# The inverse inside the recurrence, computed on 32-row diagonal blocks instead of whole 128-row matrices

## The chip, the core and the metric

One core of one Trainium2 chip. The metric is the device time of one execution in microseconds (us); three executions of the kernel before are shown. The engines are PE (TensorE), DVE (VectorE), ACT (ScalarE), POOL (GpSimd) and SP (which issues the weight loads).

## The reference, cut to what matters

The program is a two-layer model on 256 tokens of width 1024. The change touches only the first mixer, a recurrence with 8 heads of width 64:

```python
def step(S, inp):
    r_t, k_t, v_t, w_t, kk_t, a_t = inp
    sa = jnp.einsum('bhvk,bhk->bhv', S, -kk_t)
    S = (S * w_t[:, :, None, :]
         + sa[..., None] * (kk_t * a_t)[:, :, None, :]
         + v_t[..., None] * k_t[:, :, None, :])
    y = jnp.einsum('bhvk,bhk->bhv', S, r_t)
    return S, y
```

`sa` of a token depends on the `sa` of all tokens before it. Over a chunk of 128 tokens this is a linear system with a strictly triangular 128x128 matrix L for each head: sa = (I - L)^-1 rhs. The kernel computes that inverse and then works by matrix products. All else (projections, retention, gates, feed-forward, the second layer) is untouched.

## The kernel before

The 256 tokens are two chunks, n = 0 and n = 1. For each chunk, `mats` holds four masked 128x128 products of each of the 8 heads: PE makes them in two matmuls of 256 columns a head (L659, L660) into banks 0 to 3 in turn, and DVE masks each bank into `mats` (L2189). L itself in the other orientation comes from four matmuls for each half of the heads into banks 4 and 5 (L666); DVE masks them (L2197).

The inverse grows by doubling: level 0 is written down directly (DVE L2197 to L2203), and level k joins neighbouring blocks of 2^k rows to blocks of 2^(k+1). Levels 1 to 4 (`WHOLE` is 5) work on whole matrices:

- POOL masks `mats` to what level k needs, `lk` (L1253), in two halves of four heads.
- PE multiplies `lk` by `inv` into banks 4 and 5 (L678, 8 matmuls), ACT copies the result to `t1` (the helper `copy`, L1432).
- PE multiplies `invT` by `t1`, and `t1` by `invT` (L688, 16 matmuls, banks 0 to 3); DVE adds the four banks to `inv` and `invT` (L2213), 512 columns each.

Half q = 0 of the heads fills its banks before half q = 1 starts, so ACT and DVE begin on the first half while PE is at the second. Levels 5 and 6 work on blocks of 32 and 64 rows: matmuls of 32x32 and 64x64 (L700, L711, L718), copies by ACT L1534, adds by DVE L2222 and L2225.

Between the steps PE runs other work: `dense(place)` issues `quarters` of the retention projections, and a quarter is six matmuls of 128x128x512 (L443 to L445). The table `QUARTERS` gives one quarter behind each `t` step and one behind each `x` step, and five behind the start. DVE and ACT have a `dense(place)` too: ACT copies results out (L1432) and makes the rounded upper part of a weight unit (L1333), DVE the remainder (L1903), once every four quarters. In the second chunk DVE also runs a piece of the rotary embedding in each level (L2144 to L2162), in the first the angles (L2039 to L2061).

Waits on PSUM go by bank: `take` makes PE wait until the bank's last content was read, `full` makes a reader wait for PE, `emptied` waits for a reader. Each engine works through its own list in the order of the code.

## Time and profile before

| | us |
|---|---|
| median of three executions | 935.45 |
| lowest, highest | 935.07, 939.02 |
| the profiled execution | 936.12 |
| span of the profiled execution, first to last instruction | 934.3 |
| PE busy | 899.6 (96% of the span) |
| DVE busy | 678.2 (73%) |
| ACT busy | 510.9 (55%) |
| POOL busy | 81.4 (9%) |
| mean granted TensorE clock, as a share of full speed | 0.993 |

The span leaves out what lies ahead of the first and behind the last instruction (1.8 us here). A matmul of fp32 operands shows as two MATMUL rows and two LDWEIGHTS rows in the trace. "Idle before" is what the engine waited, and behind the arrow stands whose work ended that wait.

### The profile page before, as it was taken

What the parts mean: (1) busy time and instruction counts of PE and PEld (TensorE: products, weight loads), DVE (VectorE), ACT (ScalarE), POOL (GpSimd) and SP (SyncE); (2) the same over time, 40 slices, a digit from 0 to 9 for tenths busy, and PEclk for the clock granted to TensorE, in tenths of its full rate; (3) what the DMA queues carried; (4) which work ended last, traced back from release to release, by engine and by line L of the source; (5) the groups of instructions that cost most, each with busy time, mean ns of one, the idle gap of its engine ahead of it and who ended that gap; (6) DMA issues with size and microseconds to landing.
All of it is one profiled execution on the core that took longest, in us unless ns stands there. A gap on an engine that the chain in (4) does not pass through costs nothing.

```text
span 934.3 us, 14617 instructions
## 1 busy us (share of the span) xinstructions
PE 899.6 (96%) x5801; PEld 786.6 (84%) x5801; DVE 678.2 (73%) x968; ACT 510.9 (55%) x732; POOL 81.4 (9%) x83
## 2 busy tenths in 40 slices
PE   6999999999999989999999899999999998999998
PEld 5998988988888769999988699988888786878777
DVE  6688737856868678898854668787686777776665
ACT  7863332243535376665643565765565666577553
POOL 6002402300000000000000000007320000000000
PEclk9999999999999989999999999999999999999999
DMA  9543222122555455565555454552323544532231
GB/s 310 171 149 105 92 91 90 47 92 90 195 188 179 149 168 181 189 208 189 183 190 197 153 172 147 185 180 90 112 82 123 176 151 153 204 105 91 91 116 64
DMA packets 80979, 136.63 MB, mean 146 GB/s; under 512 B 3957, under 2 KB 46545, under 8 KB 80912
## 3 DMA queue, kind: packets, MB, share of 16 engines
q1 hardware_dynamic: 78800, 131.17, 42.1%
q0 software_dynamic: 2112, 4.53, 1.6%
q8 instruction: 46, 0.75, 0.3%
q14 instruction: 21, 0.17, 0.1%
HBM read 134.64 MB, written 1.05 MB: 145 GB/s over the span
## 4 chain that ended last, share of the span: by engine, by line
PE 63%; DVE 6%; ACT 6%; issue 3%; DMA 1%; DVEq 0%; ACTq 0%
PE bank L443 18%; PE bank L445 17%; PE bank L444 17%; PE bank L432 3%; DVE lower L1903 2%; ACT upper L1333 2%; PE bank L1112 1%; PE bank L917 1%; PE bank L925 1%; PE bank L1096 1%; DVE arena L2456 1%; ACT arena L1819 1%; DMA loaded<-in_ffn_w_up 1%; DMA loaded<-in_ple_gate_w 1%; ACT arena L1432 1%
## 5 line engine op out<-in xcount | busy, mean ns | idle before, releaser
L1903 DVE TENSOR_TENSOR lower<-loaded,upper 128x2048 fp32r<-128x2048 f32 x122 | 278.6, 2287 | 123.8 <-ACT upper L1333 121.7
L1333 ACT ACTIVATE upper<-loaded 128x2048 fp32r<-128x2048 f32 x122 | 231.9, 1903 | 115.3 <-PE bank L445 99.0
L443 PE MATMUL bank<-xT_upper,upper 128*128 128x256 f32 (+1 forms) x664 | 186.5, 281 | 2.7 <-DVE lower L1895 1.6
L444 PE MATMUL bank<-xT_lower,upper 128*128 128x256 f32 (+1 forms) x664 | 185.0, 279 | 0.0
L445 PE MATMUL bank<-xT_upper,lower 128*128 128x256 f32 (+1 forms) x664 | 184.9, 278 | 0.0
L443 PE MATMUL bank<-upper,xT_upper 128*128 128x512 f32 (+1 forms) x360 | 146.7, 407 | 4.6 <-DVE lower L1903 3.4
L445 PE MATMUL bank<-upper,xT_lower 128*128 128x512 f32 (+1 forms) x360 | 139.9, 389 | 0.0
L444 PE MATMUL bank<-lower,xT_upper 128*128 128x512 f32 (+1 forms) x360 | 139.3, 387 | 0.0
L443 PEld LDWEIGHTS bank<-xT_upper,upper 128*128 128x128 f32 (+1 forms) x664 | 125.1, 188 | 4.1 <-DVE lower L1895 1.8
L444 PEld LDWEIGHTS bank<-xT_lower,upper 128*128 128x128 f32 (+1 forms) x664 | 125.3, 189 | 0.2
L445 PEld LDWEIGHTS bank<-xT_upper,lower 128*128 128x128 f32 (+1 forms) x664 | 125.2, 189 | 0.1
L443 PE MATMUL bank<-upper,split_arena 128*128 128x512 f32 x296 | 120.8, 408 | 2.9 <-DVE split_arena L1968 2.1
L444 PE MATMUL bank<-lower,split_arena 128*128 128x512 f32 x296 | 117.5, 397 | 0.0
L445 PE MATMUL bank<-upper,split_arena 128*128 128x512 f32 x296 | 117.5, 397 | 0.0
L1432 ACT ACTIVATE arena<-bank 128x512 f32<-128x512 f32 (+1 forms) x83 | 46.8, 587 | 94.9 <-PE bank L678 33.2
L443 PEld LDWEIGHTS bank<-upper,xT_upper 128*128 128x128 f32 x360 | 68.1, 189 | 19.8 <-DVE lower L1903 4.5
L445 PEld LDWEIGHTS bank<-upper,xT_lower 128*128 128x128 f32 x360 | 67.7, 188 | 14.9
L444 PEld LDWEIGHTS bank<-lower,xT_upper 128*128 128x128 f32 x360 | 68.0, 189 | 12.2 <-issue 0.5
L443 PEld LDWEIGHTS bank<-upper,split_arena 128*128 128x128 f32 x296 | 56.0, 189 | 17.5 <-DVE lower L1903 2.1
L445 PEld LDWEIGHTS bank<-upper,split_arena 128*128 128x128 f32 x296 | 55.9, 189 | 13.7
L444 PEld LDWEIGHTS bank<-lower,split_arena 128*128 128x128 f32 x296 | 56.0, 189 | 12.5 <-issue 0.5
L432 PE MATMUL bank<-consts,arena 128*128 128x128 f32 (+2 forms) x333 | 49.4, 288 | 15.3 <-DMA arena<-in_norm_mix_pre 4.9
(349 smaller groups left out, 1167.9 us busy)
## 6 DMA issues: line engine op xcount, KB each, us to landing
loaded<-in_w_in SPq DMA_DIRECT2D x26, 1024.0 KB, 5.1
loaded<-in_ffn_w_up SPq DMA_DIRECT2D x22, 1024.0 KB, 5.1
loaded<-in_ssm_in_w SPq DMA_DIRECT2D x20, 1024.0 KB, 5.2
loaded<-in_ffn_w_down SPq DMA_DIRECT2D x11, 1024.0 KB, 4.9
loaded<-in_ssm_out_w SPq DMA_DIRECT2D x8, 1024.0 KB, 4.9
loaded<-in_ple_gate_w SPq DMA_DIRECT2D x8, 1024.0 KB, 5.0
loaded<-in_attn_in_w SPq DMA_DIRECT2D x8, 1024.0 KB, 5.2
loaded<-in_w_branch_ret SPq DMA_DIRECT2D x4, 1024.0 KB, 4.9
```

What stands on the lines that cost most here:

```text
L432: last = pe.transpose(ps[0:n, j * P:j * P + m], a, ident[0:m, 0:m])
L443: mm(out, a[0], b[0], start=start, stop=False)
L444: mm(out, a[0], b[1], start=False, stop=False)
L445: return mm(out, a[1], b[0], start=False, stop=stop)
L917: last = mm(ps[:, P * e:P * e + P], later[:, z % 2, e, :], const("incl"), start=True, stop=True)
L925: last = mm(ps[:, 64 * e:64 * e + 64], wT[:, n, e, :], xd[:, n, 64 * hd:64 * hd + 64], start=True, stop=True)
L1096: last = mm(ps[:, w * e:w * e + w], aqT[r, u, nh * gh * n + e, P * n:P * n + P], akT[r, u, 0:w], start=False, stop=(e == nh - 1))
L1112: last = mm(ps[:, 65 * e:65 * e + 65], aeT[:, z % 2, P * (kt_ * e + s):P * (kt_ * e + s) + P], vv[:, s, 2 * u + o, :], start=(s == 0), sto ...
L1333: A(part(upper, PARTS, n), part(loaded, LOADS, n), ACT.Copy).then_inc(uppers, 1)
L1432: empty(A(dst, ps[0:part_, 0:w], func), key)
L1819: ins = A(asb[:, z % 2, w * e:w * e + w], ps[:, w * e:w * e + w], ACT.Exp, bias=mx[:, z % 2, e:e + 1], scale=rs8[:, n, hd + e:hd + e + 1])
L1903: TT(part(lower, LOADS, n), part(loaded, LOADS, n), part(upper, PARTS, n).bitcast(F32), sub) \
```

## The change

The inverse of each diagonal block of 32 rows needs nothing outside that block. Levels 1 to 4 are now computed on these four blocks alone. `blocks` holds, for each head and packed in 32 columns each, the scratch product `bt1`, the block of L `bdiag`, and the two orientations of the inverse `binv` and `binvT`. Block b lies on partitions 32b to 32b+31 and has a PSUM bank of its own, b.

- PE: L and its transpose on the diagonal blocks come from 64 matmuls with 32 columns and 64 rows of contraction (banks 4 and 5), and they now stand ahead of the matmuls of `mats`. A level is 32 matmuls of 32x32 and then 64 of 32x32, going round the four blocks; each of the four banks is filled by its last matmul.
- DVE: two copies, two masked writes and one add of `unit` make level 0, ahead of the eight `mats` banks. A level's four adds are on 32 partitions and 512 columns each. Level 4 writes into the full-size `inv` and `invT` (`inverses`), which POOL has zeroed; levels 5 and 6 copy where they added.
- ACT: four copies of 32 partitions x 256 columns a level instead of two of 128 x 512.
- POOL: one memset of `inverses`, then the four masks of a chunk in one go, 128 x 256 each, as soon as the two copies of DVE are done.

The core of the diff:

```diff
+                ps = [take(pe, ("L", n, o), 4 + o) for o in range(2)]
+                for p in range(4):
+                    for v in range(2):
+                        for b in ROWS:
+                            for o in range(2):
+                                r = slice(64 * o, 64 * o + 64)
+                                a, x = zr[r, p, n, b], bt[r, p, n, b]
+                                last = mm(ps[o][b, 64 * p + 32 * v:64 * p + 32 * v + 32], x if v else a, a if v else x,
+                                          start=True, stop=True)
...
                 for k in range(1, WHOLE):
-                    for q in range(2):
-                        pe.wait_ge(sem("lk_ready"), 2 * (WHOLE - 1) * n + 2 * (k - 1) + q + 1)
...
-                        for e in range(4):
-                            last = mm(ps[:, P * e:P * e + P], lk[:, 4 * q + e, :], inv[:, 4 * q + e, :],
+                    pe.wait_ge(sem("lk_ready"), (WHOLE - 1) * n + k)
+                    ps = [take(pe, ("t1", n, k, b), b) for b in range(4)]
+                    for hd in range(8):
+                        for b, r in enumerate(ROWS):
+                            last = mm(ps[b][r, 32 * hd:32 * hd + 32], lk[r, k - 1, hd, :], binv[r, hd, :],
                                       start=True, stop=True)
-                        fill(last, ("t1", n, k, q))
+                            if hd == 7:
+                                fill(last, ("t1", n, k, b))
                     dense(("t", n, k))
...
+                    ps = [take(pe, ("x", n, k, b), b) for b in range(4)]
+                    for hd in range(8):
+                        for v, (a, x) in enumerate(((binvT, bt1), (bt1, binvT))):
+                            for b, r in enumerate(ROWS):
+                                c = 64 * hd + 32 * v
+                                last = mm(ps[b][r, c:c + 32], a[r, hd, :], x[r, hd, :], start=True, stop=True)
+                                if hd == 7 and v:
+                                    fill(last, ("x", n, k, b))
                     dense(("x", n, k))
...
                 for k in range(1, LEVELS):
                     if k < WHOLE:
-                        for q in range(2):
-                            copy(t1[:, 4 * q:4 * q + 4, :], ("t1", n, k, q))
+                        for b, r in enumerate(ROWS):
+                            ps = full(act, ("t1", n, k, b))
+                            empty(A(bt1[r, :, :], ps[r, 0:256].rearrange("p (a b) -> p a b", a=8), ACT.Copy), ("t1", n, k, b))
...
+                    if k < WHOLE - 1:
+                        for b, r in enumerate(ROWS):
+                            ps = full(ve, ("x", n, k, b))[r, :].rearrange("p (a v c) -> p a v c", a=8, v=2)
+                            empty(TT(blocks[r, :, 2:4, :], ps, blocks[r, :, 2:4, :], add), ("x", n, k, b))
+                        emptied(ve, *[("x", n, k, b) for b in range(4)])
...
+                pool.wait_ge(sem("diag_blocks"), 2 * n + 2)
                 for k in range(1, WHOLE):
...
+                    pool.tensor_tensor(lk[:, k - 1, :, :], bdiag, const(f"off{k}").unsqueeze(1).broadcast_to([P, 8, 32]),
+                                       ALU.mult).then_inc(sem("lk_ready"), 1)
```

PE's list at one level of the inverse, before (a row's count is in matmuls of the program):

```order
L678 MATMUL bank<-arena 128x128 x8
L443 MATMUL bank<-upper,xT_upper 128x512
L444 MATMUL bank<-lower,xT_upper 128x512
L445 MATMUL bank<-upper,xT_lower 128x512
L443 MATMUL bank<-upper,xT_upper 128x512
L444 MATMUL bank<-lower,xT_upper 128x512
L445 MATMUL bank<-upper,xT_lower 128x512
L688 MATMUL bank<-arena 128x128 x16
```

and now:

```order
L687 MATMUL bank<-arena 32x32 x32
L450 MATMUL bank<-upper,xT_upper 128x512
L451 MATMUL bank<-lower,xT_upper 128x512
L452 MATMUL bank<-upper,xT_lower 128x512
L450 MATMUL bank<-upper,xT_upper 128x512
L451 MATMUL bank<-lower,xT_upper 128x512
L452 MATMUL bank<-upper,xT_lower 128x512
L697 MATMUL bank<-arena 32x32 x64
```

The quarter of retention work between the two steps stays; the steps have four times as many, smaller matmuls.

DVE's list at the start of the first chunk, before:

```order
L1903 TENSOR_TENSOR lower<-loaded,upper 128x2048
L2189 TENSOR_TENSOR arena<-bank,consts 128x512 x8
L2197 TENSOR_TENSOR arena<-bank,consts 128x4x128 x2
L2198 TENSOR_TENSOR arena<-arena,consts 128x1024
L2201 TENSOR_TENSOR arena<-arena,consts 128x1024
L2203 TENSOR_TENSOR arena<-arena,consts 128x1024
L1903 TENSOR_TENSOR lower<-loaded,upper 128x2048
L2213 TENSOR_TENSOR arena<-arena,bank 128x512 x4
```

and now:

```order
L1914 TENSOR_TENSOR lower<-loaded,upper 128x2048
L2203 COPY arena<-bank 128x4x32
L2204 TENSOR_TENSOR arena<-bank,consts 128x4x64
L2203 COPY arena<-bank 128x4x32
L2204 TENSOR_TENSOR arena<-bank,consts 128x4x64
L2207 TENSOR_TENSOR arena<-arena,consts 128x8x64
L2213 TENSOR_TENSOR arena<-bank,consts 128x512 x8
L1914 TENSOR_TENSOR lower<-loaded,upper 128x2048
L2222 TENSOR_TENSOR arena<-bank,arena 32x8x64 x4
```

Level 0 moved from behind the eight `mats` banks to ahead of them, and shrank; the adds of a level keep their number and their 512 columns.

## Rows read from the trace of the kernel before

**Rows 1.** The page, its first line.
```profile
span 934.3 us, 14617 instructions
```

**Rows 2.** Timeline of PE (start, length, line, form, count); both chunks.
```profile
86.61 2.05 PE L678 MATMUL bank<-arena 128*128 128x128 f32 x16 [0.15 <-DVE arena L2203]
...
88.41 0.48 PE L443 MATMUL bank<-upper,xT_upper 128*128 128x512 f32 x1
...
89.89 3.73 PE L688 MATMUL bank<-arena 128*128 128x128 f32 x32
...
93.38 0.48 PE L443 MATMUL bank<-upper,xT_upper 128*128 128x512 f32 x1
...
119.90 0.69 PE L700 MATMUL bank<-arena 32*32 32x32 f32 x32 [0.49 <-DVE arena L2213]
...
159.28 2.05 PE L678 MATMUL bank<-arena 128*128 128x128 f32 x16 [0.15 <-DVE arena L2203]
...
192.53 0.69 PE L700 MATMUL bank<-arena 32*32 32x32 f32 x32 [0.46 <-DVE arena L2213]
```

**Rows 3.** Timeline of PE, levels 5 and 6 of the second chunk.
```profile
194.74 0.60 PE L711 MATMUL bank<-arena 32*32 32x32 f32 x26
195.16 0.22 PE L718 MATMUL bank<-arena 32*32 32x32 f32 x2
...
195.25 0.60 PE L718 MATMUL bank<-arena 32*32 32x32 f32 x27
195.78 0.50 PE L443 MATMUL bank<-upper,xT_upper 128*128 128x512 f32 x1
...
197.91 1.11 PE L700 MATMUL bank<-arena 64*64 64x64 f32 x16 [0.49 <-DVE arena L2225]
```

**Rows 4.** Timeline of PE, start of the second chunk.
```profile
150.14 0.72 PE L666 MATMUL bank<-arena 64*128 64x128 f32 x5
150.59 0.48 PE L659 MATMUL bank<-arena 64*128 64x256 f32 x1
150.69 0.38 PE L666 MATMUL bank<-arena 64*128 64x128 f32 x2
```

**Rows 5.** Timeline of ACT, level 5 of the second chunk.
```profile
193.23 0.78 ACT L1534 ACTIVATE arena<-bank 32x256 f32<-32x256 f32 x2 [4.96 <-PE bank L700]
```

**Rows 6.** Timeline of DVE, levels 5 and 6 of the second chunk.
```profile
196.77 0.43 DVE L2222 TENSOR_TENSOR arena<-bank,arena 32x256 f32<-32x256 f32 x1
197.23 0.42 DVE L2225 TENSOR_TENSOR arena<-bank,arena 32x256 f32<-32x256 f32 x1
...
201.81 0.68 DVE L2225 TENSOR_TENSOR arena<-bank,arena 64x512 f32<-64x512 f32 x1 [0.25 <-PE bank L718]
```

**Rows 7.** Timelines of PE and DVE, start of the first chunk.
```profile
72.78 0.71 PE L659 MATMUL bank<-arena 64*128 64x256 f32 x4
...
79.30 0.50 PE L443 MATMUL bank<-upper,xT_upper 128*128 128x512 f32 x1
...
75.15 3.67 DVE L2189 TENSOR_TENSOR arena<-bank,consts 128x512 f32<-128x512 f32 x6
```

**Rows 8.** Timelines of POOL and DVE, start of the first chunk.
```profile
80.63 3.58 POOL L1253 TENSOR_TENSOR arena<-arena,consts 128x512 f32<-128x512 f32 x2 [65.25 <-DVEq L2193]
...
83.18 2.11 DVE L2201 TENSOR_TENSOR arena<-arena,consts 128x1024 f32<-128x1024 f32 x1
85.32 1.23 DVE L2203 TENSOR_TENSOR arena<-arena,consts 128x1024 f32<-128x1024 f32 x1
```

**Rows 9.** Timeline of DVE, levels 3 and 4 of the second chunk.
```profile
184.13 0.69 DVE L2148 TENSOR_TENSOR arena<-lora 128x512 f32<-128x512 f32 x1
...
188.94 1.28 DVE L2213 TENSOR_TENSOR arena<-arena,bank 128x512 f32<-128x512 f32 x2
```

**Rows 10.** Late in the program: PE timeline; a window (length, busy by engine, PE clock, DMA).
```profile
534.58 0.50 PE L443 MATMUL bank<-upper,xT_upper 128*128 128x512 f32 x1 [2.20 <-DVE lower L1903]
...
535.90:539.30 3.40, 3.40 (x14) 2.91 (x13) 1.84 (x5) 2.21 (x5) 0.00 (x0) 0.50 0.00 0
```

More of the change, by code:

```diff
@@ L48, in constants @@
     parts["blkret"] = np.repeat(parts["blk"][:, ::64], P, axis=1)
-    for k in range(LEVELS):
-        same = (row >> (k + 1)) == (col >> (k + 1))
-        parts[f"off{k}"] = same & (((col >> k) & 1) == 1) & (((row >> k) & 1) == 0)
-    parts["off0L"] = parts["off0"].T
+    at, b = r[:, None] % 32, np.arange(32)[None, :]
+    pair = [(at >> (k + 1) == b >> (k + 1)) & ((b >> k) & 1 == 1) & ((at >> k) & 1 == 0) for k in range(WHOLE)]
+    parts["first"] = np.concatenate([(at == b ^ 1) & (at & 1 == 1), pair[0]], axis=1)
+    parts["unit"] = np.concatenate([at == b, at == b], axis=1)
+    for k in range(1, WHOLE):
+        parts[f"off{k}"] = pair[k]
+    parts["room"] = np.zeros((P, 8 * P - 32 * (3 + WHOLE)))
     lg = np.log1p(-np.exp2(-5.0 - np.arange(8)))
@@ L236, in build @@
         lor = ar(22032, 2, 256)
-        inv, invT, t1, lk = ar(23056, 8, P), ar(24080, 8, P), ar(25104, 8, P), ar(11280, 8, P)
+        inv, invT, t1, lk = ar(23056, 8, P), ar(24080, 8, P), ar(25104, 8, P), ar(11280, 4, 8, 32)
+        inverses = ar(23056, 2, 8, P)
+        blocks = ar(25104, 8, 4, 32)
+        bt1, bdiag, binv, binvT = (blocks[:, :, v, :] for v in range(4))
+        ROWS = [slice(32 * b, 32 * b + 32) for b in range(4)]
         mid = ar(25616, 8)
@@ L292, in build @@
         dtT = lora[:, 1, 0:T]
-        later = consts[:, where["off0"][0]:where["off0"][0] + 8 * P].rearrange("p (a b c) -> p a b c", a=2, b=4)
+        later = consts[:, where["first"][0]:where["first"][0] + 8 * P].rearrange("p (a b c) -> p a b c", a=2, b=4)
         ang, cosd, sind = sm(520, 4, 32), sm(648, 4, 64), sm(904, 4, 64)
@@ L660, in _ @@
                     fill(mm(ps[:, 256:512], kt[r, p, n, :], zr[r, p, n, :], start=True, stop=True), ("m", n, hd))
-                    if hd in (3, 5):
-                        o = hd // 5
-                        r = slice(64 * o, 64 * o + 64)
-                        ps = take(pe, ("L", n, o), 4 + o)
-                        for p in range(4):
-                            last = mm(ps[:, P * p:P * p + P], zr[r, p, n, 0:P], bt[r, p, n, :], start=True, stop=True)
-                        fill(last, ("L", n, o))
                 dense(("L", n))
@@ L694, in _ @@
                     w = 1 << k
-                    for key in (("x", n, k - 1, b) for b in range(2)):
-                        emptied(pe, key, ("xt", *key[1:]))
+                    if k == WHOLE:
+                        emptied(pe, *[("x", n, k - 1, b) for b in range(4)])
+                    else:
+                        emptied(pe, *[(x, n, k - 1, b) for x in ("x", "xt") for b in range(2)])
                     ps = [take(pe, ("t1", n, k, b), 4 + b) for b in range(len(pairs))]
@@ L2184, in _ @@
             for n in range(2):
+                if n:
+                    ve.wait_ge(sem("lk_ready"), WHOLE - 1)
+                    for b in range(4):
+                        full(ve, ("x", 0, WHOLE - 1, b))
+                by_pair = blocks.rearrange("p (a o) v c -> p a o v c", o=2)
+                for o in range(2):
+                    ps = full(ve, ("L", n, o))[:, 0:256].rearrange("p (a v c) -> p a v c", a=4, v=2)
+                    ve.tensor_copy(by_pair[:, :, o, 1, :], ps[:, :, 1, :]).then_inc(sem("diag_blocks"), 1)
+                    empty(TT(by_pair[:, :, o, 2:4, :], ps, bc(const("first").rearrange("p (v c) -> p v c", v=2).unsqueeze(1),
+                                                             P, 4, 2, 32), mul), ("L", n, o))
+                emptied(ve, ("L", n, 0), ("L", n, 1))
+                TT(blocks[:, :, 2:4, :], blocks[:, :, 2:4, :],
+                   bc(const("unit").rearrange("p (v c) -> p v c", v=2).unsqueeze(1), P, 8, 2, 32), add).then_inc(sem("inv_start"), 1)
                 for hd in range(8):
```

60 lines of the change are left out of this document (16 added, 44 removed).

## The prediction

> **What bounds the kernel now.** I began with the page: the span is 934.3 us [rows 1] and PE is busy for 96% of it, so time is won only where PE's own list gets shorter or its waits do. Next I read PE's timeline through the inverse [rows 2]. From the first product of level 1 to the first 32x32 matmul of level 5 it takes 119.90 - 86.61 = 33.29 us in the first chunk and 192.53 - 159.28 = 33.25 in the second. A level is a `t` step (86.61 to 88.41, 1.80), a quarter of retention work (88.41 to 89.89, 1.48), an `x` step (89.89 to 93.38, 3.49) and another quarter. Within the four levels PE waits for nobody; it waits 0.49 and 0.46 us only at their end, and 0.15 ahead of them. ACT and DVE fit behind the quarters because half of each step's banks are full while PE makes the other half. The change makes the steps short and gives up that overlap: the four banks of a step are full only at its end. So the sum has PE's gain on one side and bare evacuations on the other.
>
> The profiled execution took 936.12 us, its span and 1.82 us around it, and is 0.67 above the median of 935.45. I work on 936.12 and carry the difference to the median.
>
> **What a small matmul costs.** Where two tiles of the array are in use, 26 rows of 32x32 take 195.16 - 194.74 = 0.42 us, 16.2 ns a row [rows 3]. Where L711 hands over to L718 the two use four tiles (two row strips, two column strips each), and 11 matmul rows start between 195.16 and 195.25: 8.2 ns a row [rows 3]. Twice the tiles, half the price, so a tile needs about 32 ns for a pass and the tiles run beside each other. The change goes round four tiles, with two rows for a matmul. I take 8.2 ns; the ends are 4 and 16.2. Behind such a burst the first large matmul starts 0.12 late: 26 intervals after 195.25 is 195.66, and L443 is at 195.78 [rows 3].
>
> The Trainium skill (TensorE: Matmul & The Clock Gate, Part 3: Packing small matmuls) says that matmuls start in program order and only weight loads are pulled ahead. By that rule four tiles would be no better than two, because both passes of a matmul lie on one tile and each waits for the one before. That is rival A. Our rows disagree: L659 of head 6 starts at 150.59, before L666 rows that stand ahead of it in the list (150.69) [rows 4]. The same page (Wait — 56ns, not 53.3ns?) gives a floor of about 25 ns between starts; by it a level would pay 192 x 25 = 4.8 us, an estimate from that page. The measured 16.2 and 8.2 lie below it, so I give it 1 in 50.
>
> **A level, step by step.**
> - `t` step: 64 rows x 8.2 = 0.52, plus 0.12: 0.64, was 1.80.
> - Then PE's quarter, 1.48, beside ACT's four copies. ACT begins 0.07 behind the large matmul; two 32x256 copies take 0.78 [rows 5], about 0.40 from start to start and 0.38 for the last, so four take 1.58. With 0.26 until PE starts that is 1.91, longer than the quarter: 0.4 of it is a wait of PE. The release lies between 0.05 and 0.4.
> - `x` step: 128 x 8.2 = 1.05, plus 0.12: 1.17, was 3.49.
> - Then DVE's four adds. DVE starts 0.16 behind; a 32x256 add is 0.42 with 0.46 from start to start [rows 6], a 512-column one is 0.68 [rows 6]. Each goes to other partitions, so I take 0.68 + 0.04 for three and 0.68 for the last: 2.84. Were they as tight as the eight `mats` writes (six in 3.67, 0.60 apart [rows 7]) they would need 2.5. The release: L2225 ends at 197.65, L700 starts at 197.91 [rows 3, 6], 0.26; I take 0.3 since four banks are waited for. Sum 3.30 against a quarter of 1.48. The wait of 1.7 us is the price of the change: DVE's columns did not shrink, only its partitions.
> - Together 0.64 + 1.91 + 1.17 + 3.30 = 7.02; four levels 28.1, against 33.29 and 33.25. Gain: 5.2 + 5.2 = **10.4 us**.
>
> **Is DVE free when an `x` step ends?** From the end of the adds to the next adds there are 0.3 + 0.64 + 1.91 + 1.17 + 0.16 = 4.2 us. The heaviest load is level 3 of the second chunk, rotary pieces and a 2048-column remainder, 188.94 - 184.13 = 4.8 us [rows 9]. It is late by 0.6, and the splits beside the angles in the first chunk by perhaps as much in one level, less since POOL is done by then. **+0.9**, between 0 and 2.5. ACT's splits lie inside the 5 us between its copies and cost nothing; that cover goes if a table load meets one.
>
> **The start of a chunk.** PE now makes L first: 128 rows on eight tiles at 8.2 ns, 1.05 us. What is queued behind it is `mats`. DVE is busy until 75.15 [rows 7], then does level 0: four PSUM reads of 128 and 256 columns at 0.2 and 0.35 apart, 1.15 with the last; the add 0.69. Here POOL comes in: its masks now start right behind the two copies. Beside a POOL mask of 128x512 (1.8 us each) a DVE operation with two SBUF inputs took 2.11 where its like took 1.23 [rows 8], 0.9 more. The new masks are half as long, so 0.5. The first `mats` write ends near 75.15 + 1.2 + 0.7 + 0.5 + 0.7 = 78.3. PE filled its four banks by 72.78 + 1.05 + 1.83 = 75.7 (16 rows of 64x256 at 0.115) and stands until then, over 2 us. Four heads follow at DVE's 0.60, and the last takes 0.9: the large matmuls begin at 81.0 instead of 79.30 [rows 7]. Less the 0.15 wait that goes, +1.5; without POOL's blocking +1.0. I take +1.3 for each chunk, **+2.6**.
>
> **Rest.** Levels 5 and 6 copy instead of add: same columns, same PSUM source, 0 (down to -0.4). The memset runs on POOL while it has nothing else to do: 0. Retention work keeps its count. What is won stays won, since PE is the bound behind the recurrence as well.
>
> **Sum:** -10.4 + 0.9 + 2.6 = -6.9 us. 936.12 gives 929.2; from the median 935.45 it gives **928.5 us**, 0.7% faster. A measurement of this kernel can tell 0.5%, 4.7 us, from no change: the bounds are 930.8 and 940.1.
>
> **Rivals.**
> - A, no gain from four tiles (0.15). 16.2 ns a row makes `t` 1.16 and `x` 2.2, the level 8.6, four levels 34.3: 1.0 longer than before. With +2.6 for the starts, 935.45 + 2.0 + 2.6 = 940. For it: no run of four tiles longer than 11 rows is in the trace. Against: those 11.
> - B, the clock (0.13), the slower side. PE would stand 1.7 us in every level and over 2 at each start. Behind a wait of 2.20 us at 534.58 the granted clock was 0.50 from 535.90 to 539.30 [rows 10], that is 1.2 GHz instead of 2.4, and large matmuls took twice as long. One such drop at each start costs 1.5 to 3 us together, leaving about 931. It decides the sign if it falls in each level: the quarter behind the `t` step then takes 2.96 instead of 1.91 and the bursts 0.6 more, 1.7 x 8 = 13.3 us: 942. The quarter behind `x` has room for it. It decides from four levels on. Against: inside a level the wait is shorter than 2.2, and work surrounds it.
> - C, DVE is the bound (0.10). Adds 2.84, rotary pieces 2.7 and half a remainder 1.1 make 6.7 of 7.0 us in a level of the second chunk. Any blocking adds in full; 0.5 a level over six levels gives 931.5, the same within the measurement.
> - D, the evacuations overlap (0.12). Adds 0.60 apart, a release of 0.1 and no blocking: 0.35 + 0.2 less a level, 1.5 less at the starts: 928.5 - 4.4 - 1.5 = 922.6.
> - The forecast itself, 925 to 932, has 0.48; the floor of 25 ns, near 955, 0.02.
>
> **Numbers.** Faster by over 0.5%: 0.40 of the forecast, all of D, a little of C: 0.54. Within: 0.08, A's nearer part 0.08, C 0.08, B's mild form 0.02: 0.26. Slower: 0.20. For 8 in 10 the range goes from 923.5 to 940.
>
> **What would show it.** The small rows of `t` in about 0.5 us and of `x` in about 1.05; 16 ns says A. Idle time ahead of the `t` product, released by DVE's add, near 1.7 us in each level, and near 0.4 ahead of `x`, released by ACT; if the first is missing, D holds. At each start a wait over 2 us ahead of the fifth head's products, released by the first `mats` write. First `t` product to first L700 in 28 to 29 us. A granted clock below 1 inside the recurrence says B. I am wrong in kind if the levels got shorter and the time did not.

## The result, and the profile after

The changed kernel takes **946.48 us** (median of four runs, 944.74 to 949.90) against 935.26 for the kernel before in the same comparison: 1.0108 times as long, interval 1.0085 to 1.0131. It is 11 us slower. I had forecast 928.5, and 940.0 as the upper end of the range.

The page of the changed kernel; its own execution took 947.09 us:

```profile
span 945.3 us, 17338 instructions
...
PE 887.9 (94%) x7177; PEld 766.0 (81%) x7177; DVE 664.9 (70%) x968; ACT 513.6 (54%) x748; POOL 62.2 (7%) x76
...
q8 instruction: 57, 0.93, 0.4%
```

PE is busy for less time than before (887.9 against 899.6 us) and the span is 11.0 us longer than [rows 1]. So the small matmuls did save PE work, and PE stands more. The third line is the queue that brings PE its instructions, 57 packets of up to 16 KB; it was 46 before. (PE's rows fit: 7177 matmuls with as many weight loads are 56.1 times 256, and the 5801 of before 45.3 times.)

The timeline of PE in the first chunk, with its small matmuls renumbered: L669 makes L, L677 `mats`, L687 the `t` step, L697 the `x` step, L712 levels 5 and 6. They answer to [rows 2, 7].

```profile
74.08 1.23 PE L669 MATMUL bank<-arena 64*32 64x32 f32 x123 [0.32 <-DVE arena L2141]
77.44 0.26 PE L669 MATMUL bank<-arena 64*32 64x32 f32 x5 [2.12 <-issue]
77.62 0.71 PE L677 MATMUL bank<-arena 64*128 64x256 f32 x4
...
90.55 0.75 PE L687 MATMUL bank<-arena 32*32 32x32 f32 x64
...
93.01 1.48 PE L697 MATMUL bank<-arena 32*32 32x32 f32 x128
...
97.54 0.74 PE L687 MATMUL bank<-arena 32*32 32x32 f32 x64 [1.47 <-DVE arena L2222]
...
100.87 0.97 PE L697 MATMUL bank<-arena 32*32 32x32 f32 x90 [0.34 <-issue]
...
108.97 0.55 PE L697 MATMUL bank<-arena 32*32 32x32 f32 x40 [0.75 <-issue]
...
114.96 0.26 PE L697 MATMUL bank<-arena 32*32 32x32 f32 x9
116.03 1.21 PE L697 MATMUL bank<-arena 32*32 32x32 f32 x119 [0.81 <-issue]
...
126.20 1.11 PE L712 MATMUL bank<-arena 64*64 64x64 f32 x16 [0.53 <-DVE arena L2240]
```

The same view of the second chunk:

```profile
148.87 0.25 PE L669 MATMUL bank<-arena 64*32 64x32 f32 x5 [1.65 <-issue]
...
163.79 0.75 PE L687 MATMUL bank<-arena 32*32 32x32 f32 x64
...
170.68 0.43 PE L697 MATMUL bank<-arena 32*32 32x32 f32 x12 [3.24 <-issue]
...
176.58 0.50 PE L697 MATMUL bank<-arena 32*32 32x32 f32 x37
177.46 0.97 PE L697 MATMUL bank<-arena 32*32 32x32 f32 x91 [0.38 <-issue]
...
186.93 0.56 PE L697 MATMUL bank<-arena 32*32 32x32 f32 x41 [2.14 <-issue]
...
198.74 1.36 PE L712 MATMUL bank<-arena 32*32 32x32 f32 x32 [2.68 <-DVE arena L2228]
...
207.41 1.50 PE L712 MATMUL bank<-arena 64*64 64x64 f32 x16
```

Eight rows end with "<-issue": PE stands in the middle of a burst and no semaphore event released it. They sum to 11.4 us. Before, this stretch (60 to 215 us) had none. Look at the counts between two of them: 90 rows of L697 from 100.87, a quarter (6), a `t` step (64), a quarter (6) and 88 rows of the next `x` step make 254 rows up to 108.97. Each row goes with a weight load, so that is some 508 PE instructions, two times 256 within the few semaphore instructions that the count leaves out. The idles fall on such multiples throughout.

DVE and ACT in level 1 of the first chunk, the lines that answer to [rows 5, 6]:

```profile
94.56 2.84 DVE L2222 TENSOR_TENSOR arena<-bank,arena 32x512 f32<-32x512 f32 x4 [3.30 <-PE bank L697]
```
```profile
91.29 1.57 ACT L1540 ACTIVATE arena<-bank 32x256 f32<-32x256 f32 x4 [2.36 <-PE bank L687]
```

And windows, with the granted clock of PE as the third number from the end: first the whole recurrence of the kernel before, then of the changed one and two stretches of it.

```profile
60.00:215.00 155.00, 151.29 (x1189) 132.75 (x1188) 109.57 (x140) 55.59 (x68) 31.24 (x23) 1.00 0.27 87
```
```profile
60.00:215.00 155.00, 130.19 (x2510) 103.21 (x2509) 92.37 (x135) 54.06 (x79) 10.15 (x15) 0.91 0.27 81
...
78.50:81.90 3.40, 3.40 (x17) 2.61 (x15) 3.30 (x7) 0.00 (x0) 3.20 (x5) 0.50 0.00 0
...
198.00:208.20 10.20, 9.45 (x115) 7.14 (x116) 6.26 (x13) 3.15 (x4) 0.00 (x0) 0.50 0.26 95
```

A mean of 0.91 over 155 us is some 27 us at 0.50 (1.2 GHz); before there were none. They are five stretches, from 78.5, 150.2, 170.7, 187.7 and 198.0. PE executes 2510 matmul rows where it had 1189, in 21 us less busy time.

Where the time went, from one point of the timeline to the next:

| stretch | before | after | difference | forecast |
|---|---|---|---|---|
| first product of the chunk to level 1, first chunk (72.78 / 74.08) | 13.83 | 16.47 | +2.6 | +1.3 |
| levels 1 to 4, first chunk | 33.29 | 29.95 | -3.3 | -4.75 |
| level 5 to level 1 of the second chunk | 39.38 | 43.29 | +3.9 | +1.3 |
| levels 1 to 4, second chunk | 33.25 | 34.95 | +1.7 | -4.75 |
| level 5, second chunk (192.53 to 197.91; 198.74 to 207.41) | 5.38 | 8.67 | +3.3 | 0 |
| sum | | | +8.2 | -6.9 |

(The -4.75 is -5.2 and half of the 0.9 for DVE's lateness.) The rest of the 11.0 us is 1.3 that the profiled execution was late before the recurrence began, and 1.5 behind it. That 1.5 is no part of the change: in this execution some 800 rows more than before of the large 256-column matmuls start 117 instead of 113 ns apart, 3 to 4 us, and the clock outside the recurrence is low for 7 us less. Three of the other kernels' profiles have the 117 too; no run says where it comes from.

### The profile page after: what moved, and what is told of

Its sections match the earlier page's. It is cut to its first block, busy times and chain, and to the rows that moved or that the text cites. A ratio compares the mean times of both kernels' runs of the same rounds, so it can differ in the third digit from the quotient of the medians.

```text
span 945.3 us, 17338 instructions
## 1 busy us (share of the span) xinstructions
PE 887.9 (94%) x7177; PEld 766.0 (81%) x7177; DVE 664.9 (70%) x968; ACT 513.6 (54%) x748; POOL 62.2 (7%) x76
## 4 chain that ended last, share of the span: by engine, by line
PE 63%; DVE 6%; ACT 5%; issue 3%; DMA 1%; DVEq 0%; ACTq 0%
PE bank L450 18%; PE bank L452 17%; PE bank L451 17%; PE bank L439 3%; DVE lower L1914 2%; ACT upper L1343 2%; PE bank L1124 1%; PE bank L929 1%; PE bank L937 1%; PE bank L1108 1%; DVE arena L2471 1%; ACT arena L1830 1%; DMA loaded<-in_ffn_w_up 1%; DMA loaded<-in_ple_gate_w 1%; ACT arena L1442 1%
## 5 line engine op out<-in xcount | busy, mean ns | idle before, releaser
L1442 ACT ACTIVATE arena<-bank 128x512 f32<-128x512 f32 (+1 forms) x67 | 37.2, 584 | 63.5 <-PE bank L452 19.5
```

What stands on the lines that cost most here:

```text
L1442: empty(A(dst, ps[0:part_, 0:w], func), key)
```

## The experiments

Theory F: PE gets its instructions in blocks of 256, each takes some us to arrive, and the levels use them up faster than that. Rivals: E, the bare evacuations cost more than I had summed; K, the clock falls behind the waits for DVE. Each comparison has its own runs of the kernel before, medians 936.40 to 937.62 us. "Idles" in this table are those without a releaser, "half clock" is time at a granted 0.50, both from 60 to 225 us in the profiled execution alone. That execution is not always a typical one. For two quarters and transposed it is the fastest of ten, with a mean granted clock of 0.991 where the other nine have 0.978 to 0.987 and 0.974 to 0.989, no better than the 0.979 to 0.984 of the changed kernel: their 10 us of half clock say nothing of the medians. For half the count it is the second slowest (0.976, the others 0.980 to 0.991), for the last row the slowest.

| run | PE rows | median us | ratio to before, interval | idles us | half clock us |
|---|---|---|---|---|---|
| changed kernel | 7177 | 946.48 | 1.0085 to 1.0131 | 11.4 | 27 |
| half the count | 6409 | 935.04 | 0.9950 to 1.0004 | 4.2 | 31 |
| `t` twice | 7689 | 956.03 | 1.0192 to 1.0246 | 11.4 | 31 |
| two quarters | 7177 | 941.45 | 1.0017 to 1.0074 | 11.5 | 10 |
| before, padded | 6953 | 955.72 | 1.0188 to 1.0244 | 1.9 | 3 |
| transposed | 6665 | 935.06 | 0.9954 to 1.0011 | 2.7 | 10 |
| transposed, quarters | 6665 | 925.69 | 0.9867 to 0.9929 | 3.2 | 10 |
| L between | 7177 | 938.87 | 1.0010 to 1.0068 | 9.8 | 10 |
| before, one burst | 6313 | 952.26 | 1.0125 to 1.0212 | 6.3 | 14 |
| all three | 6665 | 926.88 | 0.9871 to 0.9940 | 7.4 | 10 |
| all three, 4 behind L | 6665 | 924.69 | 0.9857 to 0.9898 | 8.1 | 7 |
| L between, quarters | 7177 | 939.84 | 1.0016 to 1.0051 | 14.2 | 20 |

### Half the matmuls, twice the columns

```diff
-                    for hd in range(8):
+                    for hd in (0, 2, 4, 6):
                         for b, r in enumerate(ROWS):
-                            last = mm(ps[b][r, 32 * hd:32 * hd + 32], lk[r, k - 1, hd, :], binv[r, hd, :],
+                            last = mm(ps[b][r, 32 * hd:32 * hd + 64], lk[r, k - 1, hd, :], binv[r, hd:hd + 2, :],
```

(and the `x` step in the same way)

> The changed kernel with half the matmuls in levels 1 to 4: each takes the weights of the even head of a pair and streams the 32 columns of both heads of it, so 16 matmuls in place of 32 in the t step and 32 in place of 64 in the x step, with as many moving columns in all. It leaves out the products of the odd heads with their own weights (they are taken with the even head's), so its output is not the reference's. PE rows fall by 768 (7177 to 6409). Theory F (PE runs out of instructions: each block of 256 PE instructions must arrive while the one before it executes, and the levels go through one in 4.3 us): a block then lasts some 7 to 8 us, the idles inside bursts that nothing releases (sum 11.4 us in the changed kernel's profile) fall under 3 us, most of the half-clock stretches behind them go too, and the time falls by 8 to 14 us, to 932 to 939. Theory E (the waits of PE for DVE's and ACT's bare evacuations are what was mis-sized): those waits stay, so only the array's share goes, at most 384 weight loads at 8.2 ns, 3 us: 943 to 946. Theory K (the clock falls because of the evacuation waits, and the idles matter little): clock stretches stay, 942 to 946.

935.04 us, 11.4 less than the changed kernel, and 0.9977 of the kernel before. The levels in the timeline of PE:

```profile
96.91 0.65 PE L687 MATMUL bank<-arena 32*32 32x64 f32 x32 [1.45 <-DVE arena L2222]
...
116.48 0.69 PE L712 MATMUL bank<-arena 32*32 32x32 f32 x32 [1.67 <-DVE arena L2228]
...
190.12 1.06 PE L712 MATMUL bank<-arena 32*32 32x32 f32 x32 [3.25 <-DVE arena L2228]
```

Not one idle without a releaser is left in the levels, 7.2 us less; the two at the L burst (2.19 and 2.06) stay, since L was not changed. The waits for DVE stay as E says, six from 1.37 to 1.63 us. The array's share is 2.3 to 3.9 us (eight levels of a `t` step of 0.65 in place of 0.75 and an `x` step of 1.09 in place of 1.28 or 1.48), and with the 7.2 that is 9.5 to 11.1 us. The two profiled executions, 947.09 and 939.13, differ by only 8.0; the second had a granted clock of 0.976 against 0.982 over the whole, 10 us more at half clock. F holds for the idles. Of the clock it had said too much: in this execution it stays low for as long as in the changed kernel. Windows of this run:

```profile
96.00:117.00 21.00, 15.30 (x356) 11.28 (x356) 16.91 (x30) 9.29 (x18) 0.00 (x0) 1.00 0.21 71
118.30:128.50 10.20, 10.20 (x97) 7.30 (x96) 3.97 (x5) 2.64 (x3) 0.00 (x0) 0.50 0.32 104
```

Four waits of 1.4 to 1.7 us in 20 us did not lower it while they lasted; 1.8 us behind the fourth it fell for 10.2 us, in which PE was never idle.

### The t step issued twice

```diff
+                            mm(ps[b][r, 32 * hd:32 * hd + 32], lk[r, k - 1, hd, :], binv[r, hd, :], start=True, stop=True)
                             last = mm(ps[b][r, 32 * hd:32 * hd + 32], lk[r, k - 1, hd, :], binv[r, hd, :],
```

> The changed kernel with every 32-row matmul of the t step of levels 1 to 4 issued twice: 64 more PE rows a level, 512 in all, two more blocks of 256 instructions over the eight levels, all in the bursts. Theory F: a burst of the t step plus the x step is now 256 instructions without a dense quarter's cover of its own length, so the price of an added row is well above the array's: idles without a releaser grow from 11.4 us to 16 to 22, the time rises by 8 to 15 us. Theories E and K, in which rows cost only what the array takes: 512 x 8.2 ns = 4.2 us more, and the idles without a releaser stay near 11.

(512 rows and as many loads are four blocks, not two; my slip.) 956.03 us, 9.5 more: F's size. But the idles that were to grow to 16 to 22 us stayed at 11.4; they moved, an example is 1.58 us at 101.91, in the middle of a `t` step. The profiled execution, the fastest of its four, has a span 6.7 us longer than the changed kernel's. The array's 4 to 5 us explain most of that, and the rest I cannot assign: F's number came true here without its mechanism, and the run is no support for it.

### Two quarters behind each x step

```diff
-        QUARTERS[("x", _n, _k)] = 1
+        QUARTERS[("x", _n, _k)] = 2 if _k < WHOLE else 1
...
-QUARTERS.update({"R": 2, ("scores", 0): 4, ("scores", 1): 4, "o": 3, "yT": 9, "end": 8})
+QUARTERS.update({"R": 2, ("scores", 0): 4, ("scores", 1): 4, "o": 3, "yT": 7, "end": 6})
```

(and 3 in place of 5 behind L)

> The changed kernel with two quarters of dense work behind each x step of levels 1 to 4 in place of one, taken from the stretch behind L (5 to 3 for each chunk), from the output projection's stretch (9 to 7) and from the end (8 to 6). The same instructions in another order. Theory E: the wait of PE at each next t step for DVE's adds (1.4 to 1.7 us a level, six of them bare, some 9 us) is covered, and the places that gave quarters lose at most 2 x 1.5 us of cover behind L: 938 to 941. Theory F: as much, and in addition a block of 256 instructions lasts 1 us longer in the levels, so the idles without a releaser fall from 11.4 us to 5 to 9: 934 to 939. Against both: the quarters taken away from behind L bare the start of the inverse (level 0 and lk), and at the end the output work, and the time stays within 2 us of 946.5.

941.45 us, 5.0 less, just above the 938 to 941 of E and outside F's 934 to 939. In the profiled execution (934.45, the fastest) the waits for DVE in the levels go (one of 0.45 us is left), and the idles keep their sum of 11.5 us, where F had expected 5 to 9: more cover per level did not make the blocks arrive in time. At the first `mats` write DVE is now late, 1.06 and 2.26 us.

### The kernel before with padding

```diff
                         ps = take(pe, ("t1", n, k, q), 4 + q)
+                        for e in range(36):
+                            r = slice(32 * (e % 4), 32 * (e % 4) + 32)
+                            mm(ps[r, 0:32], mats[r, 4 * q, 0, r], inv[r, 4 * q, r], start=True, stop=True)
```

> The kernel before with 72 extra matmuls of 32 x 32 a level (levels 1 to 4, both chunks), 36 ahead of each quarter's t products and into the bank that these then overwrite: 1152 PE rows more, so near the changed kernel's count, with nothing else changed. Theory F: the stretches go through blocks of 256 instructions much faster, idles without a releaser inside the bursts appear at every 256th PE instruction as in the changed kernel, 8 us or more of them, and the time is 15 us or more above the kernel before. If rows cost only what the array takes, 1152 x 8.2 ns = 9.4 us more, or less where the rows fill PE's waits, without such idles: 940 to 945.

955.72 us, 19.3 more, as F asks, but not for F's reason: one idle, 1.92 us, in place of 8 us or more. A padded level takes some 9.9 us (the first chunk's four 129.59 - 89.71 = 39.88), so a block of 256 instructions lasts over 6 us and mostly arrives in time. The price is that of the rows. The padding starts at 88.96 and the product behind it at 89.71: 72 rows in 0.75, 10.4 ns a row, 12.0 us for 1152. The rest is not laid to a cause. A threshold can't be read from this: blocks of nearly 7 us end in an idle in the changed kernel, as the next run helps to see.

### One burst in the kernel before

```diff
                         ps = take(pe, ("t1", n, k, q), 4 + q)
+                        for e in range(256 if n == 0 and k == 1 and q == 0 else 0):
+                            r = slice(32 * (e % 4), 32 * (e % 4) + 32)
+                            mm(ps[r, 0:32], mats[r, 0, 0, r], inv[r, 0, r], start=True, stop=True)
```

> The kernel before with one burst of 256 extra 32 x 32 matmuls (512 PE rows, 1024 PE instructions with their weight loads: four blocks of 256) ahead of the first t product of level 1 of the first chunk, into a bank that is then overwritten, and nothing else: the price of fetching by itself. Theory F: the array's share is 512 x 10.4 ns (a row in the padded kernel's trace) = 5.3 us, but each block after the first one or two needs 3.4 to 4.2 us to arrive, so the burst lasts 11 to 16 us with idles without a releaser about 256 instructions apart, and the time rises by as much, to 947 to 952. If instructions are never missing: the burst lasts 5.3 us, 941 to 942.

952.26 us, 15.9 more, at the upper end of F's range. Timeline of PE, then the DMA view from 84 to 106 us (each digit and each GB/s figure is 0.55 us):

```profile
88.71 1.65 PE L679 MATMUL bank<-arena 32*32 32x32 f32 x172
92.55 1.93 PE L679 MATMUL bank<-arena 32*32 32x32 f32 x128 [2.18 <-issue]
96.55 1.93 PE L679 MATMUL bank<-arena 32*32 32x32 f32 x128 [2.07 <-issue]
100.55 1.39 PE L679 MATMUL bank<-arena 32*32 32x32 f32 x84 [2.08 <-issue]
101.86 3.77 PE L681 MATMUL bank<-arena 128*128 128x128 f32 x16
```
```profile
GB/s 0 0 48 112 287 406 406 413 231 4 30 0 0 0 0 0 0 0 30 0 0 0 0 0 0 30 0 0 0 0 0 0 30 0 0 0 0 0 0 0
...
q8 instruction: 4, 0.07, 1.3%
```

This is the theory by itself. Runs of exactly 128 rows, with 128 loads 256 instructions, start **4.00 us** apart (3.46 to 3.73 where the burst was later placed elsewhere and no weights were landing; there the packet starts 1.1 us after the block in place of 1.6). Between them lies one instruction packet each, the lone 30s in the second view: it starts 1.6 us after PE takes up a block (94.18 after 92.55), lasts 0.94, and the next block runs 1.43 later. So a block is asked for only when the one before it is in use, and PE has 4.0 us of work in a block or it stands.

Not all idles of the changed kernel are of this kind. Each of the eight ends 1.3 to 1.5 us after a packet has landed, so it is instructions that were missing. The packets of three (2.12, 0.75 and 1.65 us, **4.5** together) start 1.0 to 1.9 us after PE took up the block before, as in the burst. Those of the other five (0.34, 0.81, 3.24, 0.38 and 2.14, **6.9** together) start 2.8 to 4.5 us after it, at the ends of blocks that last 5 to 7 us. Two of these blocks run from idle to idle in the timelines above: 40 + 6 + 64 + 6 + 9 = 125 rows in 116.03 - 108.97 = 7.06 us, and as many in 177.46 - 170.68 = 6.78. In four of the five a landing of weights overlaps the time in which the packet was due. In the fifth none does. The DMA view of the changed kernel from 166 to 182 us (0.4 us a figure) has the end of a landing at 168.5 and then nothing until the packet at 175.13, the first 41:

```profile
GB/s 379 410 410 394 410 200 5 0 0 0 0 0 0 0 0 0 0 0 0 0 0 0 41 0 0 0 0 0 0 0 0 41 0 0 0 0 0 36 92 143
```

That packet starts 4.45 us after its block was taken up at 170.68. Eight such late packets (3.3 to 5.0 us) with no weights landing are in the profiles of seven kernels here. What holds them back is not shown.

The Trainium skill (Runtime: NRT & Kernel Launch, Instruction fetch mechanics) has the sequencer fetch instructions in blocks of 16 KiB, 256 of them, and says that crossing a boundary is mostly hidden. The trace agrees on the 256. On the hiding the measurement decides: 2.1 us at each boundary where 128 small rows are all the cover.

### One product of each mirrored pair, the other turned by DVE

```diff
-                        for v, (a, x) in enumerate(((binvT, bt1), (bt1, binvT))):
+                        for v, (a, x) in enumerate(((binvT, bt1), (bt1, binvT))[0:1 if k < WHOLE - 1 else 2]):
...
-                            empty(TT(blocks[r, :, 2:4, :], ps, blocks[r, :, 2:4, :], add), ("x", n, k, b))
+                            empty(TT(binv[r, :, :], ps[:, :, 0, :], binv[r, :, :], add), ("x", n, k, b))
+                        ve.transpose(binvT, binv).then_inc(sem("turned_back"), 1)
```

(and L made with v = 1 alone)

> The changed kernel in which the second of each pair of mirrored products is not computed on PE but turned by DVE, 32 x 32 block by block: L is computed one way only (64 PE rows a chunk in place of 128), and in levels 1 to 3 the x step computes only the inverse's product (64 rows in place of 128), DVE adds half as many columns and then turns the whole compact inverse in one instruction more. 512 PE rows less (7177 to 6665), the same result. Theory F (blocks of 256 PE instructions arrive too slowly for the bursts): a block lasts about 6 us in the levels, the idles without a releaser fall from 11.4 us to 0 to 4, and the time falls by 5 us of array work and 7 to 11 of idles, to 931 to 936. Theory E (bare evacuations): the array's 5 us alone, and DVE's evacuation of a level stays at 1.5 to 1.9 us: 940 to 943. Rows for the price: the turning instruction on DVE 0.3 to 0.5 us.

935.06 us, 11.4 less, inside F's 931 to 936. DVE's timeline in level 2 of the first chunk:

```profile
98.84 1.77 DVE L2224 TENSOR_TENSOR arena<-bank,arena 32x256 f32<-32x256 f32 x4 [0.76 <-PE bank L699]
100.75 0.45 DVE L2226 STREAM_TRANSPOSE arena<-arena 128x256 f32<-128x256 f32 x1
```

Four adds of half the columns take 1.77 in place of 2.84 us and the turning 0.45, as expected. The Trainium skill (VectorE: DVE Perf Modes, The three transpose paths) says that DVE turns 32x32 blocks only, each by itself; that is the very shape of this packing. PE waits for the adds for 0.33 to 0.41 us in five levels and 1.03 in one, so part of the gain is E's. Idles fall to 2.7 us in the profiled execution, the fastest of ten. The L burst, now 64 rows, has none, and the wait that the prediction had seen at the chunk's start appears in its place:

```profile
79.42 0.70 PE L677 MATMUL bank<-arena 64*128 64x256 f32 x2 [2.06 <-DVE arena L2215]
```

### The same with two quarters

> The kernel of the run before this one with two dense quarters behind each x step of levels 1 to 4 (behind L 3 in place of 5, output projection 7 in place of 9, end 6 in place of 8): both remedies together. If F and the clock's falls behind bare waits are both at work, this covers the evacuations and keeps the clock up: no idle over 1 us at the levels' heads, no half-clock stretch between 85 and 145 us, and 925 to 931, below the kernel before (936.5). If the second remedy gives nothing on top (the taken quarters are missed elsewhere), within 2 us of the run before this one.

(Its edit is the table's, as above.) **925.69 us, 0.9898 of the kernel before**: faster than both, in the forecast range. PE waits nowhere at the levels' heads, and the clock is first low from 143.6 us (I had asked for none up to 145). Together the two remedies give 20.8 us, alone 11.4 and 5.0; the medians' intervals, some 3 us to each side, leave open how much of the difference is the combination.

### L behind the fourth head

```diff
                 for hd in range(8):
+                    if hd == 4:
+                        pl = [take(pe, ("L", n, o), 4 + o) for o in range(2)]
...
```

(and DVE's work on L in the same place)

> The changed kernel with the products of L, and DVE's work on them, moved from ahead of the eight heads' products to behind the fourth (the kernel before had them behind the fourth and the sixth), same instructions otherwise. If DVE's work on L ahead of the first head's mask is what costs the chunk starts (predicted 1.3 us each), 943 to 945. Theory F: the L burst still meets a block's end and idles there or a little later, so no gain beyond that; the time is within 3 us of 946.5 and the sum of idles without a releaser stays between 8 and 14 us.

938.87 us, 7.6 less, where I had expected 943 to 945, and F a time within 3 us of 946.5. From the first chunk's first product to level 1 it takes 87.57 - 74.54 = 13.0 us (16.5 in the changed kernel, 13.8 before), and from level 5 to level 1 of the second chunk 158.91 - 120.02 = 38.9 (43.3, and 39.4 before). Neither L burst has an idle here, PE waits 0.16 us at most at the `mats` writes, and the low clock is 10 us in place of 27. So the place of L, with the same instructions, set the chunks' starts: 3.4 and 4.4 us, together as much as the whole gain, although 9.8 us of idles remain.

### All remedies, and the order alone

> Three remedies together: the mirrored products turned by DVE in place of computed on PE (as in the run with transposed blocks), two dense quarters behind each x step of levels 1 to 4 with 3 behind L, and L with DVE's work on it behind the fourth head's products. The run with the first two left PE waiting for DVE at the first masks, 2.07 and 2.85 us; those go, and what comes in their place is L's evacuations being 3 us later with only three quarters to cover them. If that cover is enough: 920 to 924, the fastest. If not, PE waits at level 1's head for lk by 1 to 2 us a chunk: 924 to 927.

> As the run before this one, with four dense quarters behind L (output projection 6, end 5). If the cover behind L was what that one lacked, 1 to 3 us below it; if not, it is the same within 1 us, or slower where the end misses its quarters.

> The changed kernel with the two changes of order alone and all of its PE instructions: L behind the fourth head, and two dense quarters behind each x step (3 behind L, 7, 6). Theory F: with 7177 PE rows some blocks of 256 instructions still come late, 5 to 10 us of idles without a releaser remain, and the time is 932 to 938, 8 us or more above the same order with 512 rows less. If idles were only a companion of the uncovered waits: 926 to 930.

926.88, 924.69 and 939.84 us. The first lands in the lesser of its two ranges, but not for its reason, since PE does not wait for `lk` at level 1's head: against the run without L's move (925.69) nothing is won. The waits at `mats` fell from 2.07 and 2.85 to 0.32 and 0.62 us, and the idles rose from 3.2 to 7.4. With four quarters behind L it is 924.69, **0.9877 of the kernel before**, the fastest here, though its interval overlaps with the other's. In its timeline the freed time stands at a block's end:

```profile
114.44 0.32 PE L700 MATMUL bank<-arena 32*32 32x32 f32 x3 [3.55 <-issue]
```

The order alone with all 7177 rows is no better than L's move by itself (938.87), with 14.2 us of idles, more than the 5 to 10 expected, and above the expected 932 to 938. 512 rows fewer in the same order are worth 13.0 us (939.84 to 926.88), against 4.2 to 5.3 that the array takes for them; the idles differ by 6.8. The adds on DVE were halved too, but PE waits for DVE by no more than 0.44 us in levels 1 to 4 of either profile. So the number of rows costs more than the array's time, as F says.

### Does an instruction packet wait for weights?

In the changed kernel idles of 3.24 and 2.14 us stand where 1 MB of weights was landing; the burst alone gives 2.1 with little else on PE. So the burst was moved ahead of level 1's `x` step, then its block boundaries shifted by more matmuls of the same kind ahead of the `t` step (44, then 24).

> The kernel before with the same burst of 512 extra PE rows as in the run with one burst, placed elsewhere: ahead of the x step of level 1 of the first chunk, behind its quarter of dense work, where in the kernel before a unit of weights (1 MB) lands from 91.1 to 95.3 us. The run with one burst showed a block of 256 PE instructions each 4.00 us, its 16 KB packet starting 1.6 us after PE takes up the block before, with no weights landing. If instruction packets wait for weights in flight: the first packet due within the landing starts only at its end, one block of the burst lasts 6 to 8 us in place of 4, and the burst (first to last row) lasts 2 to 4 us longer than the 13.1 us of the run with one burst. If a landing does nothing to them: all blocks again 4.0 us apart, the burst within 1 us of 13.1.

950.92 us; neither forecast came. Idles of 1.02, 3.28 and 1.80 us: blocks 4.55 and 3.73 us apart. The packet was due 1.6 us after 92.36, at 94.0, and started at 94.47; the landing ended at 94.7. Too near its end to tell.

> The run with the burst behind a landing of weights, with 44 more of the same matmuls (88 PE rows, 0.9 us) ahead of level 1's first t product, which moves the boundaries of the blocks of 256 instructions 88 rows towards the front of the burst, to its rows 61 and 189. A boundary is then crossed some 0.6 us into the burst, about when the weights begin to land, and the packet of the next block falls due 1.6 us later, 2 us or more before the landing's end. If packets wait for weights in flight: that packet starts at the landing's last 0.5 us or behind it, not in its middle, and the idle that it ends lasts 4 us or more where the run with one burst had 2.1. If a landing does nothing to them: the packet starts 1.6 us after the crossing, in the middle of the landing, and the idle is 2.0 to 2.5 us.

> The same with 24 matmuls (48 rows) in place of 44: boundaries at rows 101 and 229 of the burst, the first crossed about 1.0 us into it, the packet due 1.2 us or more before the landing's end. If packets wait: start at the landing's end, the idle about 3 us, between those of the two other placings. If not: 2.0 to 2.5 us.

953.61 and 954.49 us, from two executions each. Timeline of PE with 44 ahead, then with 24:

```profile
91.41 1.79 PE L691 MATMUL bank<-arena 32*32 32x32 f32 x189
96.19 1.27 PE L691 MATMUL bank<-arena 32*32 32x32 f32 x128 [3.00 <-issue]
```
```profile
91.36 2.12 PE L691 MATMUL bank<-arena 32*32 32x32 f32 x229
98.39 1.93 PE L691 MATMUL bank<-arena 32*32 32x32 f32 x128 [4.92 <-issue]
```

With 24, the boundary is at row 101, crossed at about 91.36 + 0.95 = 92.3. The packet was due near 93.9 and started at 95.93, at the landing's end: 2 us late, and the idle is 4.92 us, the longest of this placing, where I had said 3. (If a packet is due 1.1 us after a block is taken up, as in the later blocks of this run, it was 2.5 us late.) With 44 the packet was due at 93.6 and started at 93.98, in the landing's middle, so it did not wait; there the weights were late instead, landed 6.4 us after their issue, against 5.0. So a packet can wait for a landing to end, and one that comes early enough goes in between. The profiles of all sixteen kernels say the same. They have 236 landings of 1 MB that begin between 60 and 240 us (median 3.65 us). 87 instruction packets started between 3 us into a landing and 0.3 us behind its end, and only 17 in the first 3 us; the landings around those 17 all lasted 4.18 us or more. Which of the two it will be can't be read off beforehand.

## Why the prediction was wrong

**The step that failed** is "A level, step by step" with "The start of a chunk": every burst was priced by the array's 8.2 ns a row, as if PE always had its instructions. The change turned 1189 matmul rows of this stretch into 2510, and nothing in the sum counted instructions against their supply. That missing term measured 11.4 us in the changed kernel; the run with half the count removed 7.2 of it and the time followed. Only 4.5 of the 11.4 are blocks of 256 that PE used up in less than their 4.0 us; the other 6.9 stand behind packets that started late. The sum has 8.2 + 6.9 = 15.1 us to explain. The idles are 11.4, and the second term is the clock, at nothing in the sum: 27 us at half clock, some 9 us by the price below (an estimate). The two are more than 15.1 because they overlap with forecast waits: behind a quarter at half clock PE waits 0.16 and 0.39 us for the adds, not 1.4. The third is L's place ahead of `mats`, put at 2.6 us for both chunks: with L behind the fourth head the starts took 7.8 us less, the idles of 2.12 and 1.65 us in L's bursts among them.

- **The small matmul, 8.2 ns:** nearly right. 64 rows of `t` last 0.75 and 128 of `x` 1.28 to 1.48; without the last row's own 0.19 that is 8.6 to 10.2 ns from start to start. Rival A, which had 16.2, is out. The Trainium skill (TensorE: Matmul & The Clock Gate, Part 3: Packing small matmuls) says that matmuls start in strict program order; the price that the prediction drew from it is not in these rows.
- **ACT's copies, DVE's adds:** right to the digit where the clock and DVE were undisturbed: 1.57 (forecast 1.58) and 2.84 (2.84). PE waits 1.39 to 1.47 for the adds (forecast 1.7). In the first chunk a level was 97.54 - 90.55 = 6.99 us, forecast 7.02. That it fits so well is in part luck: the `x` step was 0.24 longer, the two evacuations 0.13 and 0.18 shorter. That level had no idle; the next three had.
- **The chunk's start, +1.3 each:** the measured +2.6 and +3.9 are over twice that. The wait ahead of the fifth head was not there, because the L burst itself stopped for 2.12 and 1.65 us at a block's end and a stretch at half clock followed (78.5 to 81.9). With a shorter L burst the forecast wait shows, 2.06 us.
- **DVE's lateness, +0.9:** PE waits for it no more than the forecast 1.7 in levels 2 to 4; ahead of level 5 it is 1.68 and 2.68, and was 0.49 and 0.46 [rows 2]. Rival C did not decide.
- **Rival B, the clock:** right in kind, not in its form. 27 us at half clock, not one stretch in each level. The stretches at 78.5, 170.7 and 187.7 begin within 1.1 us of the end of idles of 2.12, 3.24 and 2.14 us, the one at 150.2 begins 1.3 us behind the idle of 1.65 and lasts 6.8, and the one from 198.0 to 208.2 begins during the wait of 2.68. Levels 2 to 4 of the first chunk ran at full clock with waits of 1.4 in each. Its price, from the same work at either level: level 5 up to level 6's first product takes 126.20 - 120.50 = 5.70 us at full clock and 207.41 - 198.74 = 8.67 at half, 3.0 more, or 0.34 us for each us at half clock. Executions of one kernel bear this out roughly: half the count took 929.87 us at a granted 0.991 and 939.13 at 0.976.
- **Rival D and the 25 ns floor:** neither the overlap nor the floor is in the rows.
- **"I am wrong in kind if the levels got shorter and the time did not":** so it was in the first chunk, where the levels took 3.3 us less and the start gave 2.6 of it back.

What stays open: which waits bring the clock down (in its profile half the count had no idle in its levels and as much time at half clock); some 4 us by which the doubled `t` step and 7 by which the padding exceed the array's price; and what holds a packet back, above all where no weights land.

## What to carry to other kernels

Before splitting matmuls into many small ones, count PE instructions, two for each row of the trace, and compare with their supply: here 256 for every 3.5 to 4.0 us at best, so PE stands if 128 rows bring less work than that. More is no guarantee: a late packet made PE stand behind blocks of 7 us too. Look in the timeline for idles that nothing releases, at equal distances in instructions. If there are some, cut the count first (a mirrored product turned by DVE gave 11.4 us), then spread the bursts among large matmuls, and judge the two together. Look also at where a burst stands: moving one without removing a matmul gave 7.6 us. And when only one execution of a kernel is profiled, compare its time and granted clock with the others' before reading the clock from it.

## What the runs showed of the hardware

- A block of 256 PE instructions comes in one 16 KB packet of about 1 us, at best 1.1 to 1.6 us after the block before it is taken up, and is executed 1.4 us after it landed: 3.46 to 4.00 us from block to block in the bursts. In the changed kernel five of eight came 2.8 to 4.5 us after it.
- Weights in flight can delay it: by 2 us in one of three placings of a burst (4.92 us of idle), and landings in whose first 3 us a packet starts last 4.2 us or more in place of 3.65.
- 32x32 matmuls round four tiles start every 8.5 to 10.2 ns at full clock (128 rows in 1.27 to 1.48 us) and every 13.3 ns at half clock (1.93 us).
- DVE turns 128x256 values of fp32 in 32x32 blocks in 0.45 us.
